# Stacked high and low score operands, one tick a granule in the first stage, decays by transposes, alpha and beta weights side by side, in a hybrid decoder layer

## What is computed

```python
x = x + 0.5 * post(swiglu(pre(x)))            # FFN 1, width 2816
proj = pre(x) @ w_in                          # q k v z alpha beta (4 heads x 128), q k v (8 heads x 64)
o_a = gdn_mixer(...)                          # gated delta rule, chunked
o_b = dilated_mixer(qb, kb, vb)               # windows (128,1), (512,4), (2048,16), ALiBi
x = x + post(concat[o_a, o_b] @ w_out)
x = x + post(memory_cross_attention(pre(x), norm(mem)))   # 4 heads, 256 memory tokens
x = x + 0.5 * post(swiglu(pre(x)))            # FFN 2
```

## Time and profile before

| | |
|---|---|
| median of 3 runs | 2523.95 us (2523.39 to 2524.24) |
| the profiled execution's own time | 2523.32 us |
| its span | 2521.6 us, 30432 instructions |
| TensorE busy | 2484.4 us (99%) |
| VectorE, ScalarE, POOL busy | 1216.9, 919.8, 400.2 us |
| DMA, mean over the span | 110 GB/s |

### The profile page before, as it was taken

One profiled execution on the slowest core, in us unless ns is written; L12 is line 12 of the kernel. 1 busy time (PEld: TensorE's weight loads), 2 busy tenths in 40 slices (PEclk: granted clock), 3 DMA queues, 4 the chain that ended last, 5 costly groups with the idle time before them and its releaser, 6 DMA issues.

```text
span 2521.6 us, 30432 instructions
## 1 busy us (share of the span) xinstructions
PE 2484.4 (99%) x12176; PEld 2049.4 (81%) x12176; DVE 1216.9 (48%) x1927; ACT 919.8 (36%) x1435; POOL 400.2 (16%) x505
## 2 busy tenths in 40 slices
PE   7999999999999999999999999999999999999997
PEld 7888888878888887778887888788888778888886
DVE  5453334662555534467834475444553536533334
ACT  5422223432323233545424243355343424322222
POOL 1460000100222200032111242321020002100001
PEclk9999999999999999999999999999999999999999
DMA  6553333434222232244233241422343144533331
GB/s 200 168 179 109 97 99 102 150 92 127 89 62 67 67 117 84 72 154 134 76 88 123 74 134 59 134 84 75 124 129 126 55 134 155 179 100 96 97 100 68
DMA packets 318781, 276.18 MB, mean 110 GB/s; under 512 B 12784, under 2 KB 266992, under 8 KB 318128
## 3 DMA queue, kind: packets, MB, share of 16 engines
q1 hardware_dynamic: 297856, 204.56, 27.2%
q0 software_dynamic: 19744, 69.66, 8.0%
q10 hardware_dynamic: 1040, 0.00, 0.0%
HBM read 245.81 MB, written 28.38 MB: 109 GB/s over the span
## 4 chain that ended last, share of the span: by engine, by line
PE 93%; DVE 2%; issue 2%; POOL 1%; DMA 1%; ACT 1%; SPq 0%; ACTq 0%; POOLq 0%; DVEq 0%
PE acc L982 17%; PE acc L984 17%; PE acc L983 17%; PE acc L1008 9%; PE acc L1010 9%; PE acc L1009 9%; PE side L1246 2%; PE side L1141 1%; PE side L1168 1%; PE side L1061 1%; PE side L1304 1%; PE side L1336 1%; PE side L1210 1%; PE side L1229 1%; PE side L1212 1%
## 5 line engine op out<-in xcount | busy, mean ns | idle before, releaser
L1922 DVE TENSOR_TENSOR w_lo<-w_raw,w_hi 128x1024 fp32r<-128x1024 f32 x384 | 475.7, 1239 | 553.7 <-ACT w_hi L1480 552.7
L1480 ACT ACTIVATE w_hi<-w_raw 128x1024 fp32r<-128x1024 f32 x384 | 405.5, 1056 | 579.2 <-PE acc L1010 314.8
L982 PE MATMUL acc<-ha_hi,w_hi 128*128 128x512 f32 (+2 forms) x968 | 393.8, 407 | 4.4 <-DVE ha_lo L2099 3.4
L982 PE MATMUL acc<-hb_hi,w_hi 128*128 128x512 f32 (+1 forms) x968 | 377.2, 390 | 1.2 <-DVE w_lo L1922 1.2
L984 PE MATMUL acc<-hb_hi,w_lo 128*128 128x512 f32 (+1 forms) x968 | 376.6, 389 | 0.0
L983 PE MATMUL acc<-hb_lo,w_hi 128*128 128x512 f32 (+1 forms) x968 | 376.6, 389 | 0.0
L984 PE MATMUL acc<-ha_hi,w_lo 128*128 128x512 f32 (+2 forms) x968 | 372.5, 385 | 0.0
L983 PE MATMUL acc<-ha_lo,w_hi 128*128 128x512 f32 (+2 forms) x968 | 371.1, 383 | 0.0
L1008 PE MATMUL acc<-w_hi,act_hi 128*128 128x512 f32 x688 | 277.7, 404 | 0.3 <-DVE act_lo L2000 0.2
L1010 PE MATMUL acc<-w_lo,act_hi 128*128 128x512 f32 x688 | 268.5, 390 | 0.0
L1009 PE MATMUL acc<-w_hi,act_lo 128*128 128x512 f32 x688 | 268.1, 390 | 0.0
(11 more groups left out here) (382 smaller groups left out, 3323.4 us busy)
## 6 DMA issues: line engine op xcount, KB each, us to landing
w_raw<-in_ffn_w_gate SPq DMA_DIRECT2D x88, 512.0 KB, 3.7
w_raw<-in_ffn_w_up SPq DMA_DIRECT2D x88, 512.0 KB, 3.7
w_raw<-in_ffn_w_down SPq DMA_DIRECT2D x88, 512.0 KB, 3.3
w_raw<-in_w_in SPq DMA_DIRECT2D x56, 512.0 KB, 3.8
x_dram<-xbuf POOLq DMA_DIRECT2D x24, 512.0 KB, 3.0
xbuf<-x_dram POOLq DMA_DIRECT2D x24, 512.0 KB, 5.8
w_raw<-in_w_out SPq DMA_DIRECT2D x16, 512.0 KB, 3.6
w_raw<-in_mem_wq SPq DMA_DIRECT2D x16, 512.0 KB, 3.9
```

The costliest lines, as they stand in the source:

```text
L982: pe.matmul(out, hi[:, k, 0:m], xh[:, k, 0:n], start=(k == 0), stop=False)
L1480: act.activation(w_hi[:, j % RING, :], w_raw[:, j % RING, :], ACT.Copy).then_inc(w_hi_ok, 1)
L1922: dve.tensor_tensor(w_lo[:, j % RING, :], w_raw[:, j % RING, :], w_hi[:, j % RING, :].bitcast(F32), ALU.subtract).then_inc(w_lo_ok, 1)
```

## The change

- **Scores.** q and k are split into high and low parts when they leave PSUM (ScalarE high, VectorE low) and stored to DRAM in these two parts. For one head the keys are stacked, high over low, on 128 partitions, and the queries in both orders. Two F32R matmuls with 128 rows, one for each order, sum up all four products of the parts. q and k are loaded for each head (`qk_load`, six transfers), v for each pair (`v_load`), and `by_residue` runs for each head with both orders of q.
- **First stage.** `km` has one tick a granule (`KCUT[1]`, TensorE, ScalarE and VectorE alike).
- **Cumulative decays.** `spread` copies the cumulative sums in place of g, and TensorE transposes them.
- **Alpha and beta.** The low part of these weights is written beside the high part in `w_hi`; one matmul with 16 columns of weights for the high tokens and one with 8 for the low tokens take the place of three; the two row groups are added after the transpose.

```diff
-QK_PARTS = [("c", 6, 1, "ad")]
-KV_PARTS = [("c", 2, 1, "ad"), ("r", 4, TT, "adad")]
+QK_PARTS = [("c", 6, 1, "d")]
+KV_PARTS = [("c", 2, 1, "d"), ("r", 4, TT, "adad")]
...
-KCUT = {2: (3, 7), 3: (2, 5, 7)}
+KCUT = {1: (7,), 2: (3, 7), 3: (2, 5, 7)}
...
-                s = slot_stored[n % 3] if h or n < 8 else qkv_stored
-                pool.dma_start(dst, qkv_slot(h, n)).then_inc(s, 16)
+                if n >= 8:
+                    pool.dma_start(v_dram[h][n - 8], v_slot(h, n - 8)).then_inc(slot_stored[n - 8], 16)
+                    return
+                for part in range(2):
+                    dst = (q_dram if n < 4 else k_dram)[h][part][n % 4]
+                    pool.dma_start(dst, qk_slot(h, n, part)).then_inc(slot_stored[2 * (n % 2) + part], 16)
...
+            def qk_load(h, hd):
+                s = attn["qk_in0"] if hd % 2 == 0 else attn["qk_in1"]
+                p, ch = hd // 2, slice((hd % 2) * AD, (hd % 2 + 1) * AD)
+                for a in range(2):
+                    rows = slice(a * AD, (a + 1) * AD)
+                    if h == 0:
+                        pool.dma_start(keys0(hd)[rows, :], k_dram[0][a][p][ch, :]).then_inc(s, 16)
+                    else:
+                        pool.dma_start(k_asis[rows, hd % 2, :, :], k_dram[:, a, p, ch, :].rearrange("h c t -> c h t")).then_inc(s, 16)
+                for b in range(2):
+                    for a in range(2):
+                        rows = slice(a * AD, (a + 1) * AD)
+                        pool.dma_start(queries(h, hd, b)[rows, :], q_dram[h][(a + b) % 2][p][ch, :]).then_inc(s, 16)
...
+            def by_residue(hd):
+                pool.wait_ge(attn["qk_in0"] if hd % 2 == 0 else attn["qk_in1"], 96 * (AH // 2 + hd // 2 + 1))
+                pool.tensor_copy(k_class(hd), strided(flat(k_asis[:, hd % 2, :, :]))).then_inc(attn["k_class"], 1)
+                pool.tensor_copy(q_class(hd), q_asis[:, hd % 2, :, :].rearrange("p b (c r) -> p b r c", r=TT)).then_inc(attn["k_class"], 1)
...
-                        kv_load(h, 0)
-                        pool.dma_start(qbT[:, 0, :], q_dram[h][:, 0, :]).then_inc(attn["q_in0"], 16)
+                        qk_load(h, 0)
                         bias_load(h, 0)
-                        pool.dma_start(qbT[:, 1:4, :], q_dram[h][:, 1:4, :]).then_inc(attn["q_in1"], 16)
-                        kv_load(h, 1)
+                        v_load(h, 0)
+                        qk_load(h, 1)
                         bias_load(h, 1)
+                        v_load(h, 1)
...
+                        if u >= 0 and u % 4 == 2 and u // 4 + 2 < AH:
+                            pool.wait_ge(attn["scores"], h * UNITS + u + 2)
+                            qk_load(h, u // 4 + 2)
                         if u >= 0 and u % 4 == 3 and u // 4 + 2 < AH:
                             pool.wait_ge(attn["max"], (h * UNITS + u) + 1)
                             bias_load(h, u // 4 + 2)
-                        if h and u in (13, 21):
-                            by_residue(u // 8 + 1)
+                            if h:
+                                by_residue(u // 4 + 2)
...
+            def cgran_ab(op, sub):
...
+                for k in range(KT):
+                    pe.matmul(out[0:16, :], both_parts[:, k, 0:16], xh[:, k, :], start=(k == 0), stop=False)
+                    done = pe.matmul(out[0:8, :], both_parts[:, k, 0:8], xl[:, k, :], start=False, stop=(k == KT - 1))
...
-                            mm = pe.matmul(SB[3][:, hd * P:(hd + 1) * P], arena[:, G_, hd * P:(hd + 1) * P], tri_u[:],
-                                           start=True, stop=True)
+                            tr = pe.transpose(SB[3][:, hd * P:(hd + 1) * P], arena[:, G_, hd * P:(hd + 1) * P], ident[:])
...
-                        mm = pe.matmul(out[:, 0:m], qbT[rows, p, i * P:(i + 1) * P], k_ring(p)[rows, 0, 0:m], start=True, stop=True)
+                        for b in range(2):
+                            mm = pe.matmul(out[:, 0:m], queries(h, hd, b)[:, tile], keys0(hd)[:, 0:m], start=(b == 0), stop=(b == 1))
...
+                        keys = flat(k_asis[:, hd % 2, :, :])[:, (TT + i - 1) * P:(TT + i + 1) * P]
+                        for b in range(2):
+                            pe.matmul(out[:, 0:LB], queries(h, hd, b)[:, tile], keys, start=(b == 0), stop=(b == 1))
+                        for b in range(2):
+                            mm = pe.matmul(out[:, LB:TOK], q_class(hd)[:, b, i, :], k_class(hd)[:, i, :], start=(b == 0), stop=(b == 1))
...
-            for _ in range(KT):
-                cgran(ha, 2, NMEM)
+                cgran(ha, 1, NMEM)
...
+            def qk_blocks(h, n0, n1, sub):
+                for n in range(n0, n1):
+                    i = section(sub)
+
+                    def hi(i=i, n=n):
+                        act.wait_ge(pe_done, DONE[i])
+                        slot_free(act, h, 2 * (n % 2), n // 2)
+                        act.activation(qk_slot(h, n, 0), A[BANK[i] % NBANK][:], ACT.Copy).then_inc(qk_hi_ok, 1)
+                    pend[0] = hi
...
+                    def lo(i=i, n=n):
+                        dve.wait_ge(qk_hi_ok, 8 * h + n + 1)
+                        slot_free(dve, h, 2 * (n % 2) + 1, n // 2)
+                        dve.tensor_tensor(qk_slot(h, n, 1), A[BANK[i] % NBANK][:], qk_slot(h, n, 0).bitcast(F32),
+                                          ALU.subtract).then_inc(acc_dve, 1)
...
-                    dve.tensor_copy(hv(G_), bc_h(gl[:, l * 4:l * 4 + 4])).then_inc(delta["g_spread"], 1)
+                    dve.tensor_copy(hv(G_), bc_h(sm[:, 7, l * 4:l * 4 + 4])).then_inc(delta["g_spread"], 1)
...
+                        link(dve.tensor_tensor(ab, SB[0][:, 0:64].rearrange("p (l e) -> p l e", e=16)[:, :, 8:16], ab, ALU.add))
```

More of the change, by code:

```diff
@@ L238, in hybrid_layer @@
         cT = at("cT", [P, 12, TOK], CZ)
+        cT_r = at("cT_r", [P, 12, TOK], CZ, F32R)
+        arena_r = at("arena_r", [P, 16, TOK], AR, F32R)
+        stage_r = at("stage_r", [P, 8, TOK], OT, F32R)
         zT = at("zT", [P, GH, TOK], CZ + 24 * K)
@@ L345, in hybrid_layer @@
         z_ok = sem("z_ok")
-        qkv_stored = sem("qkv_stored")
-        slot_stored = [sem(f"slot_stored{k}") for k in range(3)]
+        qk_hi_ok = sem("qk_hi_ok")
+        slot_stored = [sem(f"slot_stored{k}") for k in range(4)]
         kv_made = sem("kv_made")
@@ L363, in hybrid_layer @@
         attn = {n: sem("a_" + n) for n in (
-            "distance", "log_count", "q_in0", "q_in1", "kv_in0", "kv_in1", "bias_in0", "bias_in1", "scores", "max",
+            "distance", "log_count", "qk_in0", "qk_in1", "v_in0", "v_in1", "bias_in0", "bias_in1", "scores", "max",
             "neg_max", "probs", "pT_psum", "pT_sbuf", "out_psum", "out_sbuf", "outT_psum", "outT_sbuf",
@@ L454, in vm_of, with qk_slot, v_slot, slot_free @@
             return vm_all[:, :, hd * MD:(hd + 1) * MD] if h else vm_ring[:]
[L456 to L464, removed]
+        STAGING = ((4, 5, 6, 0), (1, 3, 7, 8))
+        def qk_slot(h, n, part):
+            return (stage_r, arena_r)[h][:, STAGING[h][2 * (n % 2) + part], :]
+        def v_slot(h, tt):
+            return (stage_of[0], arena)[h][:, STAGING[h][tt], :]
+        def slot_free(eng, h, k, uses):
+            if uses:
+                eng.wait_ge(slot_stored[k], 16 * (5 * h + uses))
         def staged(eng, h):
[L468 to L471, removed]
+            for k in range(4):
+                eng.wait_ge(slot_stored[k], 80 * (h + 1))
         block = ctx.enter_context(nc.Block())
@@ L1027, in gdn_in @@
             def gdn_in(op, sub):
-                for j in range(13):
-                    cgran(op, sub, TOK, 8 if j == 12 else P)
+                for _ in range(12):
+                    cgran(op, sub)
+                cgran_ab(op, sub)
             def z_in(op, sub):
@@ L1239, in pv @@
                     pe.wait_ge(attn["pT_sbuf"], n + 1)
+                    if u % 8 == 0:
+                        pe.wait_ge(attn["v_in0"] if p % 2 == 0 else attn["v_in1"], 32 * h + (64 if h else 16) * (p // 2 + 1))
                     if h == 0:
-                        groups = [[v_ring(p)[:, c, ch] for c in range(i + 1)]]
+                        groups = [[v_ring(h, p)[:, c, ch] for c in range(i + 1)]]
                     else:
-                        groups = [[v_ring(p)[:, TT + i - 1 + c, ch] for c in range(2)], [vs_ring(p)[:, c, i, ch] for c in range(2)]]
+                        groups = [[v_ring(h, p)[:, i + c, ch] for c in range(2)], [vs_ring(p)[:, c, i, ch] for c in range(2)]]
                     for a, values in enumerate(groups):
```

110 lines of the change are left out of this document (57 added, 53 removed).

## The result

The changed kernel takes 2487.3 us (median of 4 runs, 2485.6 to 2491.4), against 2523.9 us for the kernel before (4 runs): a ratio of 0.9857, 95% interval 0.984 to 0.9874. It is faster by 36.6 us; the forecast was 45.4 us faster, 2478 us, with a range of 2468 to 2492 us. The profiled execution is the longest of the four: 2491.36 us of its own, a span of 2489.6 us, so in the spans 32.0 us are gained.

What follows compares the result with a forecast made beforehand. TensorE was taken as the bound, busy 2484.4 of 2521.6 us. Gains of 52.4 us less losses of 7.0 gave 45.4 net, from the profiled 2523.3 us to 2478 us; range 2468 to 2492 us.

Steps and rivals of the forecast that it cites:

- Scores, first half: First half's attention: 29.9 us of fp32 score products and late matmuls become 12.1 us of F32R; gain 17.8 us.
- The rival by which the 0.2 us would stay: Scores: the late matmul's 0.2 us belongs to something else than rows; 12.8 us less gained, 2491 us; chance 0.05.
- Scores, second half: Second half's attention: score products and late matmuls go from 40.2 to 17.3 us; gain 22.9 us.
- the prediction's own sign: It is wrong if, among other signs, the stretches with scores are not some 18 and 22 us shorter.
- the 1.0 us for VectorE held by POOL's copies: Second half's attention: longer POOL copies hold VectorE, so probabilities come late to their transposes; loss 1.0 us.
- the rival in which POOL's copies become a second bound: Residue copies hold `w_lo` or VectorE's maxima beyond their slack at six later heads; 12 us lost, 2490 us; chance 0.17.
- The 19 us between a head's loads and their use: Later heads: issue 3.9, landing 5.5, copies 4.1 and a wait of 1.8 us fit, some 4 us to spare.
- Start of the second half: First score there waits 3.5 us for POOL's loads and copies, plus 1.7 us of clock; loss 5.2 us.
- Cumulative decays: Per chunk, four transposes at 0.44 us replace four fp32 matmuls at 0.89; gain 3.6 us over eight chunks.
- Alpha and beta: Their granule goes from 24 to 16 matmuls in each half, 3.6 us gained; the added VectorE sum loses 0.4 us.
- First stage: One tick a granule ends the 2.8 us `xbuf` wait and 1.7 us of lost clock; gain 4.5 us.

Runs made afterwards that it cites:

- e_rows64: The changed kernel with its score products over partitions 0 to 63 alone, leaving out the partial products with the keys' low part: 2509.5 us, ratio 0.9944.
- b_rows128: The kernel before with its score products over all 128 partitions, each score then summing two heads: 2502.6 us, ratio 0.9917.
- e_both: The changed kernel, second half's first q/k loads and head 0's copies ahead of v loads, copies of heads 4 and 6 held for the merge: 2478.8 us.
- after_again: The changed kernel run again, unedited: 2487.7 us, ratio 0.9859 of the kernel before.
- e_loads: The changed kernel with q and k of both first heads and head 0's copies ahead of v's loads, second half alone: 2482.4 us, ratio 0.9838.
- e_dfix: e_both, with a chunk's key and query products waiting for the subtraction that last reads their bank, not the instruction after: 2477.4 us, ratio 0.9819.
- e_act: e_loads with the residue copies of heads 2 to 7 made by ScalarE in place of GpSimd: 2485.2 us, ratio 0.9851.

## Why the prediction was right where it was, and what failed

**Scores, first half: 17.8 us predicted, 17.8 measured, with its parts mis-sized.** I charged 12.8 us of both halves to passages between 64 and 128 rows at one 0.2 us a unit, on the way out. The runs showed that the way in costs 0.14 us as well, so rows are 10.5 us of the first half's 17.8 in place of 6.4, and the type is some 7.3. The sum came right since I took the old pairs from their total, which held the 0.14: it says nothing for my split of it. The rival by which the 0.2 us would stay is out: e_rows64 brings it back and b_rows128 removes it without touching the type. "TensorE: Matmul & The Clock Gate", the page of the Trainium skill on which it rested, says in its table "Why this matters for your kernels" (not in its Part 3, which has the loads of weights) that a single matmul of 32 rows takes the same time as one of 128. For the second product of a unit, with its like ahead of it, it holds: 0.43 us with 64 rows and with 128, in this chain of b_rows128:

```profile
1739.68 0.49 PE side L1212 x2
1740.17 0.43 PE side L1214 x2
1740.60 0.23 PE acc L982
```

At each change of the row count it does not, by 0.34 us a unit.

**Scores, second half: 22.9 us less 1.0 predicted, 12.7 measured, 22.0 without the two disturbances.** By the prediction's own sign, a stretch some 22 us shorter, this half is a miss. The products cost what I said (0.53 us a unit and no late matmul, predicted 0.54). The step that failed is the 1.0 us for VectorE held by POOL's copies. I looked at `w_lo` and at the probabilities, which have microseconds to spare, and overlooked the merges: a chain of small VectorE operations with TensorE waiting at its end. Two of six later copy pairs met it and cost 4.6 us, and the clock, which was at its lower level from 1698.7 to 1702.1 us behind the second of these waits, another 1.7. That is the rival in which POOL's copies become a second bound, with two places in place of six: its mechanism was real, though the operations were not the `w_lo` and maxima that it named, and its 12 us were too many. How many merges are met is a matter of the execution: each one met is some 2 us of wait. The 19 us between a head's loads and their use were long enough at every later head: TensorE never waits for POOL there.

**Start of the second half: 5.2 us lost predicted, 6.4 measured** (4.3 of wait; the clock stays at its lower level until 1603.1 us, and the first two units take 2.1 us more than in e_both). In after_again it is 5.9, with 1.6 for the clock. The step was right and the wait 0.8 us small: the last copy took 3.00 us, not 2.1, as VectorE held it in turn. e_loads shows that it was avoidable.

**Cumulative decays: 3.6 us predicted, 1.6 measured.** The step that failed is that saved TensorE time in a chunk is all gain. VectorE's chain from the transposes to `decay_exp` did not get shorter, so TensorE came to it 0.5 to 0.8 us early in three chunks. VectorE's timeline of the changed kernel shows the two instructions; the bank is free after the first:

```profile
646.25 0.68 DVE L2255 TENSOR_TENSOR arena<-side,sm 128x512 f32<-128x512 f32 x1
646.96 0.69 DVE L2256 SCALAR_TENSOR_TENSOR arena<-arena 128x512 f32<-128x512 f32 x1
```

e_dfix, which waits for the first, got 1.7 us back, for waits of 2.0.

**Alpha and beta: 3.6 less 0.4 predicted, 2.5 measured.** The matmuls last what I took them for (392 and 393 ns with 8 and 16 weight columns). The transposes behind the shorter granule now wait for ScalarE's eviction, 0.8 us in the second half (last row of the first fence), and I had priced only the added sum.

**First stage: 4.5 us predicted, 4.55 measured after a fast start, 2.6 in the first profile.** The working holds (no `xbuf` wait, clock 1.00 from 20 to 65 us). What I did not know is that the start itself has two speeds, by which the edit is worth 4.5 or 1.0 us. No run shows what decides between them.

**The last 1.0 us.** The last matmul starts 33.0 us earlier (2507.02 and 2474.00), the end only 32.0. It is not lost in TensorE's last results or in their stores: the last store is issued 5.5 us behind the start of the last matmul, in place of 5.9.

```profile
2512.89 0.53 POOL L922 DMA_DIRECT2D out_x<-xbuf  x1 [1.52 <-DVE xbuf L2492]
...
2479.52 0.53 POOL L958 DMA_DIRECT2D out_x<-xbuf  x1 [1.17 <-DVE xbuf L2566]
```

From there to the end it is 10.1 us in place of 8.7. The trace has one long record in it, the closing DRAIN of POOL's queue, of 6.8 us in the changed kernel and its versions and 5.0 in the kernel before and b_rows128. POOL issues 295 transfers in the former and 199 in the latter; whether that is the reason, no run here shows.

Added up by the table of stretches: 1.9 us are missing from the start, 0.8 from the first half's chunks, 0.9 ahead of the second's, 2.3 between there and its first score, 7.5 in its attention and 1.0 at the end; the other stretches gave 1.0 more than predicted. That is the 13.4 us between 45.4 and 32.0. In the medians 8.8 us are missing, since the profiled execution was the longest run.

## What to carry to other kernels

When a change gives GpSimd more work, look for short dependent chains on VectorE whose end TensorE awaits, not for the large operations with slack: a copy of 2 us makes an operation of 0.17 us take 1.9. When it takes work from TensorE in front of a chain of another engine, only the part above that chain's length is gained, and it pays to check that the wait is on the last reader of the buffer and not on a later instruction. Ahead of the first product of a stage, order the transfers by who waits for them, as each issue costs half a microsecond and more.

## What the runs showed of the hardware that was not expected

- A score pair among full-row matmuls costs 0.14 us more on the way into 64 rows and 0.20 on the way out, in true fp32 and in F32R alike (1.05 and 0.43 against 0.91 and 0.23; 0.66 and 0.43 against 0.52 and 0.23).
- POOL and VectorE hold each other: a VectorE operation on 128x16 took 1.77 to 1.99 us in place of 0.17 beside a POOL copy, one on 128x1024 2.95 in place of 1.22, and POOL's copy 3.00 in place of 2.02. Beside ScalarE's copies of the same size (e_act) the merges' operations took their 0.17 and 1.22 us. The kernel loses by it where two operations of one short chain are held: 1.7 to 2.4 us of TensorE at a merge.
- TensorE began at 1.2 GHz behind some 10 us without work in all 13 profiles. It was at 2.4 GHz for the matmuls from 15 us on in 6 of them, only from 19.2 to 19.5 us on in 5, and in 2 it was fast, slow from 16.3 us and fast again from 19.7; the code of TensorE up to there differs in the ticks alone. The column of granted clock reads 1.00 for 15 to 20 us in the 5, ahead of the trace's first record of the clock; the distance between matmuls, 0.21 us for 256 columns, shows the level.
- POOL's closing DRAIN took 6.8 us in every profile of a kernel in which POOL had issued 295 transfers, and 5.0 in both with 199.
